# Attention of the second block: two heads of a pair in one body, with alternating matmuls

## What is computed

```
for branch in (selected, window):          # 16 heads, 512 queries, 512 keys, causal
    logits = q @ k[branch, group].T + rel_bias[head]     # q already scaled
    p      = softmax(where(key <= query, logits, -inf))
    out   += gate[branch] * (p @ v[branch, group])
out += gate[compressed] * (softmax(q @ k_cmp.T + bias) @ v_cmp)
```

## Time and profile before

| | |
|---|---|
| median of 3 runs | 2158.85 us (2153.08 to 2159.8) |
| span of the profiled execution | 2157.7 us, 24223 instructions |
| PE (matmul) busy | 1988.7 us (92%) |
| PEld (weight load) busy | 1578.3 us (73%) |
| VectorE (DVE) busy | 1118.0 us (52%) |
| ScalarE (ACT) busy | 713.2 us (33%) |
| GpSimd (POOL) busy | 776.9 us (36%) |
| mean granted TensorE clock | 0.939 |

### The profile page before, as it was taken

One profiled execution on the slowest core, in us unless ns is written; L12 is line 12 of the kernel. 1 busy time (PEld: TensorE's weight loads), 2 busy tenths in 40 slices (PEclk: granted clock), 3 DMA queues, 4 the chain that ended last, 5 costly groups with the idle time before them and its releaser, 6 DMA issues.

```text
span 2157.7 us, 24223 instructions
## 1 busy us (share of the span) xinstructions
PE 1988.7 (92%) x8716; PEld 1578.3 (73%) x8716; DVE 1118.0 (52%) x1798; ACT 713.2 (33%) x1162; POOL 776.9 (36%) x323
## 2 busy tenths in 40 slices
PE   7947775999999799999999999999799999999997
PEld 5735453788888578788888888888566678888885
DVE  6988837744434654435443346522755526433444
ACT  5244343322222342133222223232366543222221
POOL 3343031444344334344454444443000024444442
PEclk9987886999999899999999999978599999999998
DMA  4211021232233223783333332322000112333231
GB/s 168 79 39 40 10 68 30 84 101 90 96 97 98 78 68 106 118 195 108 98 98 101 93 94 92 108 82 80 10 20 20 55 39 85 96 112 95 80 98 59
DMA packets 52167, 177.32 MB, mean 82 GB/s; under 512 B 5527, under 2 KB 5911, under 8 KB 52088
## 3 DMA queue, kind: packets, MB, share of 16 engines
q1 hardware_dynamic: 47952, 166.22, 24.3%
q10 hardware_dynamic: 4136, 10.02, 3.3%
HBM read 166.75 MB, written 9.47 MB: 82 GB/s over the span
## 4 chain that ended last, share of the span: by engine, by line
PE 78%; DVE 3%; issue 1%; ACT 0%; DVEq 0%
PE ps L372 24%; PE ps L373 24%; PE ps L374 24%; PE ps L462 4%; PE ps L453 2%; PE ps L695 1%; DVE rstd L1186 0%; PE ps L426 0%; DVE arena L1549 0%; DVE h L1822 0%; DVE arena L1766 0%; DVE arena L1463 0%; PE ps L673 0%; PE ps L661 0%; PE ps L638 0%
## 5 line engine op out<-in xcount | busy, mean ns | idle before, releaser
L339 POOL TENSOR_TENSOR WL<-raw,WH 128x1024 fp32r<-128x1024 f32 x301 | 751.5, 2511 | 1329.9 <-ACT WH L724 1329.9
L372 PE MATMUL ps<-XH,WH 128*128 128x512 f32 (+1 forms) x1296 | 513.9, 397 | 63.8 <-DVE XL L1191 32.8
L374 PE MATMUL ps<-XH,WL 128*128 128x512 f32 (+1 forms) x1296 | 509.4, 393 | 0.0
L373 PE MATMUL ps<-XL,WH 128*128 128x512 f32 (+1 forms) x1296 | 509.4, 393 | 0.0
L724 ACT ACTIVATE WH<-raw 128x1024 fp32r<-128x1024 f32 x301 | 310.0, 1053 | 548.9 <-PE ps L374 499.8
L372 PE MATMUL ps<-HH,WH 128*128 128x512 f32 x1056 | 421.2, 399 | 34.9 <-DVE arena L1335 16.7
L373 PE MATMUL ps<-HL,WH 128*128 128x512 f32 x1056 | 417.1, 395 | 0.0
L374 PE MATMUL ps<-HH,WL 128*128 128x512 f32 x1056 | 416.6, 395 | 0.0
L372 PEld LDWEIGHTS ps<-XH,WH 128*128 128x128 f32 x1296 | 252.7, 195 | 125.6 <-issue 51.1
L374 PEld LDWEIGHTS ps<-XH,WL 128*128 128x128 f32 x1296 | 252.6, 195 | 50.0
L373 PEld LDWEIGHTS ps<-XL,WH 128*128 128x128 f32 x1296 | 253.1, 195 | 49.0 <-issue 0.7
(11 more groups left out here) (191 smaller groups left out, 1753.4 us busy)
## 6 DMA issues: line engine op xcount, KB each, us to landing
raw<-in_weights SPq DMA_DIRECT2D x301, 512.0 KB, 3.6
tab<-arena ACTq DMA_DIRECT2D x1, 5120.0 KB, 77.7
arena<-tab SPq DMA_DIRECT2D x16, 256.0 KB, 2.7
ftab<-arena ACTq DMA_DIRECT2D x1, 2080.0 KB, 23.7
h<-in_xT SPq DMA_DIRECT2D x8, 256.0 KB, 8.2
out_T<-h SPq DMA_DIRECT2D x8, 256.0 KB, 2.1
arena<-ftab ACTq DMA_DIRECT2D x4, 256.0 KB
arena<-in_pT ACTq DMA_DIRECT2D x1, 512.0 KB, 3.5
```

What stands on the lines that cost most here:

```text
L339: nc.gpsimd.tensor_tensor(WL[:, s, :], raw[:, s, :], WH[:, s, :].bitcast(f32), SUB)\
L372: nc.tensor.matmul(out, wh, xh, start=start, stop=False)
L373: nc.tensor.matmul(out, wh, xl, start=False, stop=False)
L374: return nc.tensor.matmul(out, wl, xh, start=False, stop=stop)
```

## The change

Sixteen bodies take the place of the 32 jobs. A body is one branch of both heads of a pair (`Pair`). In `pair_scores` and `pair_values` each matmul of the head on partitions 0 to 63 is followed by the same one of the head on 64 to 127; in the scores the two write different PSUM banks, in the values different partition halves of bank 6. Transposes are not alternated: head 0, then head 1. PE's order in a body is the scores of steps 0 and 1 (blocks 0, 1 and block 2), values of two bodies back, the scores of step 2 (block 3), transposes of the body before. VectorE alternates logits of the new body with reciprocals and scalings of the one before. It writes the negated logits and takes their minimum, so the negation of the maxima goes; Exp gets scale -1. The gate is the second factor of the four scalings, so the product of reciprocal and gate goes. ScalarE waits for each block of logits rather than for the whole job. There are four probability buffers for three and four bias strips for three; the fourth strip waits until the compressed branch no longer reads its space. GpSimd's loop of weight splits is cut in two loops at the attention, with the units in the same order. The diff without the removed bodies that stand above:

```diff
--- before.py
+++ after.py
-        strips, PB2, PT2, O2 = cut(8192, 3, S), cut(9728, 3, 1280), cut(13568, 2, 1280), cut(0, DC, S)
+        strips, O2 = cut(8192, 4, S), cut(0, 2, S)
+        PB2 = [cut(x, 1280) for x in (1024, 2304, 10240, 11520)]
+        PT2 = [cut(x, 1280) for x in (13568, 14848)]
...
+        class Pair:
+            def __init__(self, n):
+                self.pair, self.br = divmod(n, 2)
+                self.g = 2 * self.pair // HG
+                self.heads = (2 * self.pair, 2 * self.pair + 1)
+                self.half = (slice(0, 64), slice(64, 128))
+            def p(self, n, r):
+                return PB2[2 * (n % 2) + r]
+            def value(self, kt):
+                at = self.br * 256 + HD * self.g
+                return V2[:, kt, at:at + HD]
         KEYS = [4 * br + g for g in range(GR) for br in range(2)]
-        JOBS2 = [job2(n) for n in range(2 * H2)]
+        PAIRS = [Pair(n) for n in range(H2)]
+        STEPS2 = ((0, 1), (2,), (3,))
+        LOGITS2 = (4, 6, 8)
...
             for hd in range(H2):
-                if hd < 3:
+                if hd < 4:
                     sp.wait_ge(sems["kr_lo"], 2)
-                else:
-                    sp.wait_ge(sems["l_done"], 4 * H1 + 8 * (hd - 2))
-                sp.dma_start(strips[:, hd % 3, :], bass.AP(io["tab"].tensor, hd * 640 * P + 127, [[639, P], [1, S]]))\
-                  .then_inc(strip_in[hd % 3], 16)
+                    if hd == 3:
+                        sp.wait_ge(sems["lt_ok"], GR)
+                elif hd % 2 == 0:
+                    sp.wait_ge(sems["l2_done"], 16 * (hd // 2 - 1))
+                sp.dma_start(strips[:, hd % 4, :], bass.AP(io["tab"].tensor, hd * 640 * P + 127, [[639, P], [1, S]]))\
+                  .then_inc(strip_in[hd % 4], 16)
...
-            for n in range(NJ + 3):
-                if n < NJ:
-                    if n % (2 * HG) == 0:
+            def pair_scores(n, step):
+                job, c = PAIRS[n], 3 * n + step
+                if c >= 2:
+                    k, before = divmod(c - 2, 3)
+                    pe.wait_ge(sems["l2_done"], 8 * k + LOGITS2[before])
+                else:
+                    pe.wait_ge(*m["tile_free"].upto())
+                for qs in STEPS2[step]:
+                    w, at = P * (qs + 1), P * (qs == 1)
+                    for k, (low, of) in enumerate(((XH, HH), (XH, HL), (XL, HH))):
+                        for r in range(2):
+                            x = job.half[r]
+                            last = nc.tensor.matmul(ps[:, 2 * (c % 2) + r, at:at + w],
+                                                    low[x, job.pair, qs * P:(qs + 1) * P], of[x, job.br * GR + job.g, 0:w],
+                                                    start=k == 0, stop=k == 2)
+                last.then_inc(sems["s2_done"], 1)
+            def pair_transposes(n, r):
+                j = 2 * n + r
+                pe.wait_ge(sems["n2_done"], 4 * (j + 1))
+                for g, group in enumerate(TRANSPOSES):
+                    if j:
+                        pe.wait_ge(*((sems["pt_g0"], j) if g == 0 else (sems["pt_rest"], 2 * (j - 1) + g)))
+                    for kt, qs, at in group:
+                        last = nc.tensor.transpose(ps[:, TBANK[g], at:at + P],
+                                                   PAIRS[n].p(n, r)[:, POFF[qs] + kt * P:POFF[qs] + (kt + 1) * P], ident[:, :])
+                    last.then_inc(sems["t2_done"], 1)
+            def pair_values(n):
+                job = PAIRS[n]
+                out = [ps[x, 6, :] for x in job.half]
+                if n == 0:
+                    pe.wait_ge(*m["kc_lo"].upto())
+                if job.br == 0:
+                    if job.pair:
+                        pe.wait_ge(sems["pv_out"], job.pair)
+                    for r in range(2):
+                        i = job.heads[r] % HG
+                        nc.tensor.matmul(out[r], VC[32 * i:32 * i + 32, HD * job.g:HD * job.g + HD],
+                                         PCT[32 * i:32 * i + 32, job.g, :], start=True, stop=False, skip_group_check=True)
+                for g, kts in enumerate(VALUES):
+                    if g == 0:
+                        pe.wait_ge(sems["pt_g0"], 2 * n + 2)
+                    else:
+                        pe.wait_ge(sems["pt_rest"], 4 * n + 2 + g)
+                    for kt, at in kts:
+                        for r in range(2):
+                            last = nc.tensor.matmul(out[r][:, kt * P:S], job.value(kt), PT2[r][:, at:at + S - kt * P],
+                                                    start=False, stop=job.br == 1 and (g, kt) == (2, 2), skip_group_check=True)
+                last.then_inc(sems["pv_done"], 1)
+            for n in range(NP + 2):
+                if n < NP:
+                    if n % HG == 0:
                         pe.wait_ge(*m["krep_lo"].next(2))
-                    scores(n, JOBS2[n])
+                    pair_scores(n, 0)
+                    pair_scores(n, 1)
+                if n >= 2:
+                    pair_values(n - 2)
                 if n == 0:
                     compressed_transposes()
...
+                if n < NP:
+                    pair_scores(n, 2)
+                if 1 <= n <= NP:
+                    for r in range(2):
+                        pair_transposes(n - 1, r)
...
+            def pair_exp(n, r, qs, k):
+                act.wait_ge(sems["l2_done"], 8 * n + k)
+                a = PAIRS[n].p(n, r)[:, POFF[qs]:POFF[qs] + P * (qs + 1)]
+                c = 8 * (n % 2) + 4 * r + qs
+                nc.scalar.activation(a, a, ACT.Exp, bias=small[:, NMX + c:NMX + c + 1], scale=-1.0,
+                                     accum_out=small[:, SUM + c:SUM + c + 1]).then_inc(sems["e2_done"], 1)
+            def pair_copy(n, r):
+                for g, (at, w) in enumerate(((0, S), (S, S), (2 * S, 256))):
+                    act.wait_ge(sems["t2_done"], 3 * (2 * n + r) + g + 1)
+                    nc.scalar.activation(PT2[r][:, at:at + w], ps[:, TBANK[g], 0:w], ACT.Copy)\
+                      .then_inc(sems["pt_rest" if g else "pt_g0"], 1)
             def pair_out(pair):
-                nc.scalar.activation(O2[:, pair, :], ps[:, 6, :], ACT.Copy).then_inc(*m["o_out"].tick())
-            for n in range(NJ + 2):
-                if n >= 2:
-                    copy_transposed(n - 2, JOBS2[n - 2])
-                if n >= 6 and n % 4 == 2:
-                    pair_out((n - 6) // 4)
-                if n < NJ:
-                    exponentials(n, JOBS2[n], 1.0)
+                act.wait_ge(sems["pv_done"], 2 * pair + 2)
+                nc.scalar.activation(O2[:, pair % 2, :], ps[:, 6, :], ACT.Copy).then_inc(sems["pv_out"], 1)
+                act.wait_ge(sems["pv_out"], pair + 1)
+                nc.scalar.activation(XH[:, pair, :], O2[:, pair % 2, :], ACT.Copy).then_inc(*m["x_hi"].tick())
+            for n in range(NP + 2):
+                if n < NP:
+                    for k, (r, qs) in enumerate(((0, 0), (0, 1), (1, 0), (1, 1), (0, 2), (1, 2))):
+                        pair_exp(n, r, qs, k + 1)
+                if 1 <= n <= NP:
+                    pair_copy(n - 1, 0)
+                if n < NP:
+                    pair_exp(n, 0, 3, 7)
+                    pair_exp(n, 1, 3, 8)
+                if 1 <= n <= NP:
+                    pair_copy(n - 1, 1)
+                if n >= 3 and n % 2 == 1:
+                    pair_out((n - 3) // 2)
...
-            for n in range(NJ + 1):
-                if n < NJ:
-                    hd = n // 2
+            def pair_logits(n, step):
+                job, c = PAIRS[n], 3 * n + step
+                dve.wait_ge(sems["s2_done"], c + 1)
+                for r in range(2):
+                    for qs in STEPS2[step]:
+                        w, at, k = P * (qs + 1), P * (qs == 1), NMX + 8 * (n % 2) + 4 * r + qs
+                        V.tensor_tensor_reduce(out=job.p(n, r)[:, POFF[qs]:POFF[qs] + w],
+                                               in0=ps[:, 2 * (c % 2) + r, at:at + w],
+                                               in1=strips[:, job.heads[r] % 4, S - w:S], scale=-1.0, scalar=3.0e38,
+                                               op0=ADD, op1=ALU.min,
+                                               accum_out=small[:, k:k + 1]).then_inc(sems["l2_done"], 1)
+            def pair_inverse(n, r):
+                k = 8 * (n % 2) + 4 * r
+                dve.wait_ge(sems["e2_done"], 8 * n + 7 + r)
+                V.reciprocal(small[:, INV + k:INV + k + 4], small[:, SUM + k:SUM + k + 4]).then_inc(sems["i2_done"], 1)
+            def pair_normalise(n, r):
+                dve.wait_ge(sems["i2_done"], 2 * n + r + 1)
+                for qs in range(TT):
+                    a = PAIRS[n].p(n, r)[:, POFF[qs]:POFF[qs] + P * (qs + 1)]
+                    k = INV + 8 * (n % 2) + 4 * r + qs
+                    gate = 3 * PAIRS[n].heads[r] + 1 + PAIRS[n].br
```

(30 more changed lines are left out.)

54 lines of the change are left out of this document (14 added, 40 removed).

## The result

| | kernel before | changed kernel |
|---|---|---|
| median of the runs | 2159.32 us (2153.08 to 2161.37, 4 runs) | 2087.94 us (2087.02 to 2098.86, 4 runs) |
| ratio | 1 | 0.9707 [0.9671, 0.9743] |
| span of the profiled execution | 2157.7 us | 2085.2 us |
| attention stage, first logits to projection | 204.55 us | 145.06 us |
| from the end of the stage to the end | 408.8 us | 408.8 us |

The account below looks back on a forecast made before the run. PE's issue order was taken to bound the attention stage (204.5 us); filling, fourteen bodies at 9.4 us and a last of 6.2 gave 159, 45.5 less, so 2113 us. Range 2088 to 2148, likeliest case 2091 to 2125.

Parts of the forecast that it names:

- the step on which the forecast rested: PE's array works on both halves at once, so a body's PE sum is 8.95 us against 12.28; chance 0.58.
- Scores, put at 2.7 us with 0.3 for the changes of kind: PE, both heads' scores per body: 2.7 us, between 2.10 and 4.20; four changes between matmul kinds at 0.08 add 0.3.
- under that I let no alternating pair come: PE scores: each matmul costs at least 0.11 us in issue, so an alternating pair takes at least 0.22.
- Values 2.7, compressed pair 1.5: PE: both heads' values 2.30 plus 0.4 us; compressed pair three steps instead of four, 1.5 us every second body.
- The long loop: Every second body, from ScalarE's second copies through bank 6, PE's products and Exp to the next second copies: 10.6 us.
- The other bodies: Bodies without the compressed pair: loop 7.8 us, so PE's own sum decides, 8.2 us; mean of both kinds 9.4.
- the lower case of its range: All loads hidden, products at one head's time: loop 9.5, other bodies 7.9 by ScalarE, mean 8.7, stage 148, 56 us less.
- its own signs: PE's timeline: scores 2.5 to 3 us, 512-column pairs within 0.24, values under 3, bodies 8.7 to 10 apart, alternating.
- Filling and draining: Stage's ends: first values some 21 us behind the first logits, last body 6.2 us, around fourteen bodies at 9.4.
- (a): Rival: only the scores overlap, values stay 4.6 us; PE 11.1 us per body, stage 187, 17 us less, 2142; chance 0.22.
- (b): Rival: nothing overlaps and the new order stalls; 12.3 to 12.9 us per body, 4 to 15 slower, about 2170; chance 0.15.
- (c): Rival: PE's new waits hold the clock at its lower level; 16 us per body, 54 us slower, 2213; chance 0.05.

Follow-up runs that it names:

- The experiment with the early copy: Changed kernel with ScalarE copying bank 6 out right behind a body's first four Exp: 2087.04 us, ratio 0.9685; repeated over six runs 2080.68 us, ratio 0.9669.
- the values experiment: Changed kernel with the compressed product and the values issued head by head, not alternating: 2134.15 us, ratio 0.9917.
- parting both halves: Changed kernel with the upper half's score, compressed and value matmuls waiting on a semaphore for the lower half's last: 2182.61 us, ratio 1.013.

## Why the prediction came out as it did

That the halves work at once was the step on which the forecast rested, and it held: pairs start 0.01 us or less apart. The size of the gain was off, since a part of the parallel work was withheld in the sum.

- **Scores, put at 2.7 us with 0.3 for the changes of kind.** Measured 1.43 + 0.90 = 2.33 with the changes (1619.86 to 1621.29, 1623.59 to 1624.49). The step that was off is "under that I let no alternating pair come". From a distance of 0.11 between two matmuls of one half I inferred a cost of issue of the engine, and doubled it. But a pair starts every 0.11 too: the 0.11 belongs to a half.
- **Values 2.7, compressed pair 1.5.** Measured 2.30 and 1.00. The 0.4 and 0.5 us for seams between the halves are not there. Values and compressed pair lie at the lower end of the bounds, the scores 0.2 us above it (they now stand in two groups, so change kind twice), and what the Trainium skill says there (TensorEngine Tiling (Array Packing), Key Properties: tiles run in parallel) holds here without a discount. By it the body's PE work was to be 7.7 us; the trace has 7.18 in a body without the compressed pair (7.85 less the wait of 0.67) and 1.00 more with it, 7.7 on average.
- **The long loop, put at 10.6.** It closes as written, from ScalarE's copies to the next ones, 1611.14 to 1620.55: copies and bank 6 with hand-over 1.87, pair 1.00, values 2.31, scores of step 2 0.89, up to the first copy 0.69, copies 1.24, two Exp 1.41, in all 9.41. Of the 1.2 us too much, 0.9 are the two discounts above and 0.5 the Exp and copies, which I took one by one and which overlap in a row; against them step 2 took 0.2 more.
- **The other bodies, put at 8.2 by PE's sum.** 7.85, and not PE's sum: PE waits 0.67 us for VectorE's second scalings. The loop there is VectorE's, from the logits of step 0 to the end of the second scalings, then transposes and scores. The experiment with the early copy agrees: it shortens the longer body to 8.27 and leaves this one at 7.85. The prediction had named this outcome as the lower case of its range: 9.5 for the loop, 7.9 for the others, mean 8.7, stage 148. The loop's 9.5 came by the mechanism given there. The 7.9 was put down to ScalarE, and that the measured 7.85 is so near is luck. Of its own signs, two came out short: scores at 2.33 us (2.5 to 3 were to show it) and every second body at 7.85 (8.7 to 10).
- **VectorE and ScalarE.** The scalings take 1.51 us a head, as forecast; by one column they would gain nothing. The wait at bank 6 is where it was put, 1.16 us in the second body of each two, and moving the copy takes 12 us off the stage.
- **The sum.** Fourteen bodies at 9.4 - 8.67 (17.35 / 2) are 10.2 us. Filling and draining was put at 27.4 and took 145.06 - 14 x 8.67 = 23.7, 3.7 more. Together 13.9 of the 14.0 us by which the stage came out under the forecast 159. The rest, up to the 71 us, is the early start of these executions; with six and eleven runs the gain was 57.6, about the stage's.
- **The rivals.** (a), values without overlap, is what the values experiment made, 184.8 us for the stage (187 by the sum): the price came near, the case did not. A part of the nearness is luck, as the sum has 22.2 us for two bodies, the trace 21.5 at clock 1.00, and a clock of 0.93 over the stage made up for it. (b) is what parting both halves made: slower than before by 1.3%, 28 us rather than 4 to 15, with added waits and a lower clock in it; at clock 1.00 its mean body is 13.1 us, for the 12.3 to 12.9 there. (c) did not come: clock 1.00 in the steady part with 29% of a mean body in transposes (2.5 of 8.67 us), so the rule of the Trainium skill that they don't count as being busy (TensorE: Matmul & The Clock Gate, Part 4) changed nothing here. But "a slow PE has no gaps, so it would rise again" is no safe argument: in the kernel before the clock was 0.91 from 1600 to 1620 us with PE busy for 20.00 of the 20. Strips and GpSimd's loop cost nothing, as put.

Open: what the rest of the change costs by itself, to better than some tenths of a us a body. The parted kernel's bodies at clock 1.00 bound it, but they hold waits of their own, and a small overlap. Open too is what moves the granted clock ahead of the stage.

## What to carry to other kernels

Where two matmul streams each use half of the rows, or half of the columns, issue them next to each other: the second was free here, and the distance measured in one half was no cost of issue to be doubled. When a body of PE's work gets shorter by nearly a third, look at once for what waits behind the other engines' hand-written order; here one copy put in an earlier place gave a further 12 us. Price a stage by its own ends in the trace, since its start moved by up to 14 us between executions, and compare bodies at one clock, since 14.14 and 19.0 us stood for the same body in one trace.

## What the runs showed of the hardware

- Matmuls of a free half start ahead of others that the program issues earlier: with six of one head issued before six of the other, the other's first starts with the third (1602.09). The reach was three matmuls in each place seen: there, with eight value matmuls of each head in a row (3.86 us for 2.30 with alternation and 4.60 without overlap), and in the kernel parted by waits (1611.08).
- It did not reach from the values of one half to the compressed product of the other (32 rows): 3.30 us for each head, no overlap.
- The halves overlap fully with fp32 (values, halves of columns) and with fp32r (scores, halves of rows), 128 to 512 columns: sixteen value matmuls in 2.30 us as eight, a pair of score matmuls of 512 columns in 0.23 us as one.
- PE's busy share does not tell the granted clock: 0.91 with PE never idle (before, 1600 to 1620 us), 1.00 with PE idle for a tenth (after, 1550 to 1660 us).
- GpSimd's work on SBUF is not always free for VectorE: beside a subtraction of 1.30 us VectorE lost 0.96, and beside a copy of 0.61 us nothing. Idle GpSimd time next to a busy VectorE is worth less than it looks.
